# Six layers on one core: the latent attention layer computed with tokens on partitions

## What is computed

```
def mla_mixer(xn, positions, w_in, q_lat_norm, kv_lat_norm, w_uq, w_ukv, q_norm, k_norm, w_out):
    cq, ckv, kr, z = jnp.split(xn @ w_in, cuts, axis=-1)      # widths 384, 256, 32, 1024
    q = (rmsnorm(cq, q_lat_norm) @ w_uq).reshape(bsz, seq, 16, 96)
    kv = (rmsnorm(ckv, kv_lat_norm) @ w_ukv).reshape(bsz, seq, 16, 64 + 64)
    k_nope, v = kv[..., :64], kv[..., 64:]
    k = jnp.concatenate([k_nope, broadcast(kr)], axis=-1)     # 64 + 32 = 96
    q, k = rmsnorm(q, q_norm), rmsnorm(k, k_norm)
    # rope on the last 32 of the 96 of q and of k
    o = dense_chunk_attention(q, k, v, 96 ** -0.5)            # key chunk of 64 <= query chunk
    return (o * jax.nn.silu(z)) @ w_out
```

## Time and profile before

| | |
|---|---|
| median of 3 runs | 1074.57 us |
| profiled execution, its own time | 1076.47 us |
| its span, first to last instruction | 1074.7 us |
| mean granted TensorE clock | 0.954 of full |
| TensorE busy | 994.5 us (93%) |
| VectorE busy | 647.7 us (60%) |
| ScalarE busy | 496.2 us (46%) |
| GpSimd busy | 337.5 us (31%) |
| DMA | 148.5 MB, mean 138 GB/s |

### The profile page before, as it was taken

One profiled execution on the slowest core, in us unless ns is written; L12 is line 12 of the kernel. 1 busy time (PEld: TensorE's weight loads), 2 busy tenths in 40 slices (PEclk: granted clock), 3 DMA queues, 4 the chain that ended last, 5 costly groups with the idle time before them and its releaser, 6 DMA issues.

```text
span 1074.7 us, 17517 instructions
## 1 busy us (share of the span) xinstructions
PE 994.5 (93%) x7143; PEld 920.9 (86%) x7143; DVE 647.7 (60%) x1000; ACT 496.2 (46%) x668; POOL 337.5 (31%) x270
## 2 busy tenths in 40 slices
PE   6999958988869999988999999899999999999798
PEld 5999947677759988855999999899999997988698
DVE  5777535895585553558367665878665544555632
ACT  5553335444674345237244345334445236474521
POOL 7442652441122110713044323866401100222400
PEclk9999979999989999659999999899999999999998
DMA  9884424324222324503249553445464552424400
GB/s 252 211 224 167 155 76 173 128 108 157 79 82 100 119 62 133 164 6 79 57 122 234 169 215 126 157 143 190 179 235 157 194 206 78 157 86 150 157 1 40
DMA packets 128022, 148.49 MB, mean 138 GB/s; under 512 B 12835, under 2 KB 83760, under 8 KB 127952
## 3 DMA queue, kind: packets, MB, share of 16 engines
q1 hardware_dynamic: 127248, 146.32, 42.4%
q0 software_dynamic: 448, 1.12, 0.4%
q10 hardware_dynamic: 256, 0.07, 0.0%
HBM read 146.44 MB, written 1.05 MB: 137 GB/s over the span
## 4 chain that ended last, share of the span: by engine, by line
PE 61%; DVE 8%; ACT 6%; POOL 3%; issue 2%; DVEq 0%; ACTq 0%; POOLq 0%
PE acc L1557 39%; PE aux L1557 21%; POOL arena L1428 1%; DVE wlo L812 1%; ACT whi L444 1%; POOL arena L1429 1%; POOL arena L1427 1%; ACT arena L470 1%; DVE wlo L831 1%; DVE score L1109 1%; DVE work L1153 1%; DVE top L1108 1%; ACT work L656 1%; DVE arena L918 1%; ACT work L663 0%
## 5 line engine op out<-in xcount | busy, mean ns | idle before, releaser
L812 DVE TENSOR_TENSOR wlo<-raw,whi 128x2048 fp32r<-128x2048 f32 (+5 forms) x128 | 286.3, 2264 | 138.1 <-ACT whi L436 136.1
L1557 PE MATMUL acc<-xh,whi 128*128 128x256 f32 (+1 forms) x1208 | 346.4, 287 | 7.8 <-DVE wlo L812 4.2
L1557 PE MATMUL acc<-xh,wlo 128*128 128x256 f32 (+1 forms) x1208 | 343.6, 284 | 0.0
L1557 PE MATMUL acc<-xl,whi 128*128 128x256 f32 (+1 forms) x1208 | 343.6, 284 | 0.0
L436 ACT ACTIVATE whi<-raw 128x2048 fp32r<-128x2048 f32 (+5 forms) x128 | 207.5, 1653 | 107.8 <-PE aux L1557 60.4
L1557 PEld LDWEIGHTS acc<-xh,whi 128*128 128x128 f32 (+1 forms) x1208 | 233.1, 193 | 10.2 <-issue 5.8
L1557 PEld LDWEIGHTS acc<-xl,whi 128*128 128x128 f32 (+1 forms) x1208 | 233.2, 193 | 0.0
L1557 PEld LDWEIGHTS acc<-xh,wlo 128*128 128x128 f32 (+1 forms) x1208 | 233.0, 193 | 0.0
L1557 PE MATMUL aux<-yh,whi 128*128 128x256 f32 x352 | 99.9, 284 | 0.0
L1557 PE MATMUL aux<-yl,whi 128*128 128x256 f32 x352 | 99.6, 283 | 0.0
L1557 PE MATMUL aux<-yh,wlo 128*128 128x256 f32 x352 | 99.6, 283 | 0.0
(11 more groups left out here) (293 smaller groups left out, 1784.3 us busy)
## 6 DMA issues: line engine op xcount, KB each, us to landing
raw<-in_a_w_in SPq DMA_DIRECT2D x52, 512.0 KB, 6.6
raw<-in_sb_w_in SPq DMA_DIRECT2D x48, 512.0 KB, 5.6
raw<-in_b_w_in SPq DMA_DIRECT2D x36, 512.0 KB, 5.5
raw<-in_pool_w_in SPq DMA_DIRECT2D x32, 512.0 KB, 6.0
raw<-in_a_w_out SPq DMA_DIRECT2D x16, 512.0 KB, 5.0
raw<-in_pool_w_out SPq DMA_DIRECT2D x16, 512.0 KB, 5.2
raw<-in_sb_w_out SPq DMA_DIRECT2D x16, 512.0 KB, 5.0
raw<-in_c_w_in SPq DMA_DIRECT2D x12, 512.0 KB, 5.6
```

Source lines behind the costliest of these rows:

```text
L812: TT(wlo[b][:, lo:hi], (raw_third if third else raw[b])[:, lo:hi], whi[b][:, lo:hi].bitcast(F32), ALU.subtract).then_inc(lo_ready, 1)
L1557: return nc.tensor.matmul(out_, lhsT, rhs, start=start, stop=stop, skip_group_check=True)
```

## The change

The latent layer is computed with tokens on partitions. The latents (C0 with the columns 336 to 671, C0+1 with 0 to 335) come out as 128 tokens by 336 columns; squares are summed along rows by the accumulator of ScalarE; the factors are one number per partition; ten transposes bring the normed latents back to feature-major, where they are the stationary operand for k, v and q. The up-projections are eight events of 512 columns (four heads of k and v) and eight of 384 (four heads of q), token block by token block. ScalarE evacuates the first token block and VectorE the second; squares on ScalarE, sums by head with a reduction on VectorE, Ln and Exp in place of the square root; GpSimd applies the factor of k, writes the shared rotary part into every head and does the rope of q. Sixteen groups of four transposes bring k and q to 96 rows by 256 tokens, with the gain applied in the copy out. The heads take the paired form of the sparse layer (`paired_heads` for both); the last four groups of transposes, the second half of z (C0+7) and half of the first output unit stand between them as fillers, and the splits of the two output units are spread over them by quarters. The layer has 10 units for 14. The second angle table and its two constants, the rotation matrices and the first 128 KB broadcast of the positions go; two small gain loads and nine small operations on GpSimd come.

The core of the diff. The counterpart on VectorE of ScalarE's part has the same order and is not shown; what is removed can be seen in the functions above.

```diff
-A0, B0, C0, A1, P0, S0, END = 0, 10, 22, 36, 46, 62, 78
+A0, B0, C0, A1, P0, S0, END = 0, 10, 22, 32, 42, 58, 74
...
-        shapes = {B0 + 1: (8, 72), C0 + 2: (8, 160)}
-        for u in range(C0 + 4, C0 + 8):
-            shapes[u] = (2, 512)
-        for u in range(C0 + 8, C0 + 12):
-            shapes[u] = (3, 384)
+        shapes = {B0 + 1: (8, 72), C0: (8, 336), C0 + 1: (8, 336), C0 + 3: (2, 2048), C0 + 4: (3, 768),
+                  C0 + 5: (3, 384), C0 + 6: (3, 384)}
...
+        MLA_SPLITS = {first + q: (u, q) for first, u in ((2, C0 + 8), (11, C0 + 9)) for q in range(4)}
...
-            plain(C0, w, 0, 0)
-            plain(C0 + 1, w, 0, 672)
-            plain(C0 + 2, w, 0, 512)
-            plain(C0 + 3, w, 0, 1184)
-            for n in range(4):
-                plain(C0 + 4 + n, a["c_w_ukv"][0], 0, 512 * n)
-            for n in range(4):
-                plain(C0 + 8 + n, a["c_w_uq"][0], 0, 384 * n)
+            plain(C0, w, 0, 336)
+            plain(C0 + 1, w, 0, 0)
+            plain(C0 + 2, w, 0, 672)
+            plain(C0 + 3, a["c_w_ukv"][0], 0, 0)
+            plain(C0 + 4, a["c_w_uq"][0], 0, 0)
+            plain(C0 + 5, a["c_w_uq"][0], 0, 768)
+            plain(C0 + 6, a["c_w_uq"][0], 0, 1152)
+            plain(C0 + 7, w, 0, 1184)
             for h in range(2):
-                plain(C0 + 12 + h, a["c_w_out"][0], 4 * h, 0)
+                plain(C0 + 8 + h, a["c_w_out"][0], 4 * h, 0)
...
+            split(C0 + 2, (0,))
+            for t in range(NT):
+                latent_square(t, t, 48, 304, 0)
+            for t in range(NT):
+                latent_square(t, t, 304, 336, 1)
+            root(2, log=True)
+            for t in range(NT):
+                latent_square(t, t, 0, 48, 2)
+            split(C0 + 2, (1,))
+            act.wait_ge(unit_done, C0 + 2)
+            for t in range(NT):
+                latent_square(t, 2 + t, 0, 336, 3)
+            log_root(lms[:, :], lfac[:, :], "lat_ms", 1, "lat_root")
+            split(C0 + 3, (0,))
+            act.wait_ge(sem("lat_f"), 1)
+            A(lat[:, 0, 384:640], acc[:, 0, 48:304], ACT.Copy, scale=lfac[:, 0:1])
+            A(krs[:, 0, :], acc[:, 0, 304:336], ACT.Copy, scale=rT[:, 4:5])
+            A(lat[:, 0, 336:384], acc[:, 0, 0:48], ACT.Copy, scale=lfac[:, 2:3])
+            A(lat[:, 0, 0:336], acc[:, 2, 0:336], ACT.Copy, scale=lfac[:, 2:3]).then_inc(sem("lat_a"), 1)
+            split(C0 + 3, (1,))
...
+            split(C0 + 4)
             silu(40, 4, 3)
...
+            nc.scalar.preload_act_table_set("natural_log_exp_and_others")
+            for c in range(4):
+                name, count = kv_signal(2 * c)
+                act.wait_ge(sem(name), count)
+                src = c_bank(2 * c).rearrange("p (h d) -> p h d", d=128)
+                h = 4 * (c % 2)
+                A(kfull[2 * (c // 2)][:, h:h + 4, 0:64], src[:, :, 0:64], ACT.Copy).then_inc(sem("k_raw_a"), 1)
+                A(vC[:, 0, 256 * c:256 * c + 256].rearrange("p (h d) -> p h d", d=64), src[:, :, 64:128], ACT.Copy)\
+                    .then_inc(sem("kv_out_a"), 1)
+                for t in range(NT):
+                    e = 2 * c + t
+                    act.wait_ge(sem("k_raw_v" if t else "k_raw_a"), c + 1)
+                    if e >= 4:
+                        act.wait_ge(sem("k_summed"), e - 3)
+                    A(k_square(e).rearrange("p (h d) -> p h d", d=64), kfull[2 * (c // 2) + t][:, h:h + 4, 0:64],
+                      ACT.Square).then_inc(sem("k_squared"), 1)
+                if c == 2:
+                    log_root(c_heads(0, 1, 0), c_heads(1, 1, 0), "k_ms", 1, "k_root")
...
+            for c in range(4):
+                name, count = q_signal(2 * c)
+                act.wait_ge(sem(name), count)
+                h, g = 4 * (c % 2), c // 2
+                src = c_bank(8 + 2 * c)[:, 0:W384].rearrange("p (h d) -> p h d", d=96)
+                A(qraw[2 * g][:, h:h + 4, :], src, ACT.Copy).then_inc(sem("q_out_a"), 1)
                 for t in range(NT):
...
+                    act.wait_ge(sem("q_out_v" if t else "q_out_a"), c + 1)
+                    if c:
+                        act.wait_ge(sem("q_summed"), 2 * c - 1 + t)
+                    A(work[:, 4 + t, :].rearrange("p (h d) -> p h d", d=96), qraw[2 * g + t][:, h:h + 4, :], ACT.Square)\
+                        .then_inc(sem("q_squared"), 1)
+                if c == 0:
+                    log_root(c_heads(0, 1, 1), c_heads(1, 1, 1), "k_ms", 2, "k_root")
+                if c == 1:
+                    split(C0 + 6)
+                if c == 2:
+                    log_root(c_heads(0, 0, 0), c_heads(1, 0, 0), "q_ms", 1, "q_root")
+                    turn_copy(0)
+                    turn_copy(2)
+            turn_copy(4)
+            log_root(c_heads(0, 0, 1), c_heads(1, 0, 1), "q_ms", 2, "q_root")
+            turn_copy(6)
+            turn_copy(8)
+            turn_copy(10)
+            split(C0 + 7)
+            softmax_heads(1)
...
+            pool.wait_ge(sem("lat_a"), 1)
+            pool.wait_ge(sem("lat_v"), 1)
+            sin = c_tab[:, 1, 1, :, :]
+            TT(krt[:, :, 0:16], krs[:, :, 16:32], sin[:, :, 0:16], ALU.mult)
+            me.link(TT(krt[:, :, 16:32], krs[:, :, 0:16], sin[:, :, 16:32], ALU.mult))
+            me.link(TT(krs[:, :, :], krs[:, :, :], c_tab[:, 1, 0, :, :], ALU.mult))
+            me.link(TT(krs[:, :, :], krs[:, :, :], krt[:, :, :], ALU.add))
+            for g in range(2):
+                pool.wait_ge(sem("k_factor"), g + 1)
+                for t in range(NT):
+                    k, f = kfull[2 * g + t], c_heads(1, 1, g)[:, t, :].rearrange("p (h d) -> p h d", d=1)
+                    TT(k[:, :, 0:64], k[:, :, 0:64], f.broadcast_to([P, 8, 64]), ALU.mult)
+                    TT(k[:, :, 64:96], over_heads(krs[:, t, :]), f.broadcast_to([P, 8, 32]), ALU.mult)\
+                        .then_inc(sem("k_done"), 1)
+            for g in range(2):
+                for t in range(NT):
+                    pool.wait_ge(sem("q_squared"), 4 * g + 3 + t)
+                    q = qraw[2 * g + t][:, :, 64:96]
+                    cos, sin = c_tab[:, 0, 0, t, :], c_tab[:, 0, 1, t, :]
+                    TT(qturn[:, :, 0:16], q[:, :, 16:32], over_heads(sin[:, 0:16]), ALU.mult)
+                    me.link(TT(qturn[:, :, 16:32], q[:, :, 0:16], over_heads(sin[:, 16:32]), ALU.mult))
+                    me.link(TT(q, q, over_heads(cos), ALU.mult))
+                    TT(q, q, qturn[:, :, :], ALU.add).then_inc(sem("q_done"), 1)
+                    pool.wait_ge(sem("q_done"), 2 * g + t + 1)
...
+            def mla_filler(f):
+                if f < 2:
+                    turn_heads(12 + 2 * f)
+                    turn_heads(13 + 2 * f)
+                if f in (5, 6, 8, 9):
+                    if f == 5:
+                        taken("turn_out_v", 7)
+                        taken("turn_out_a", 8)
+                    unit(C0 + 7, in_tiles(1), xh, xl, part=(2 * (5, 6, 8, 9).index(f), 2))
+                if f in (12, 13, 15, 16):
+                    if f == 12:
+                        taken("z_raw", 4)
+                    attention_out(C0 + 8, 16, (12, 13, 15, 16).index(f), 0)
+            def turn_heads(i):
+                if 4 <= i < 12:
+                    taken("turn_out_v" if i % 2 else "turn_out_a", (i - 4) // 2 + 1)
+                elif i > 12:
+                    taken(*((), ("turn_out_a", 6), ("turn_out_v", 6), ("turn_out_a", 7))[i - 12])
+                g = i % 8 // 4
+                o, src = turn_bank(i), (kfull if i < 8 else qraw)[2 * g:2 * g + 2]
+                for n in range(2):
+                    for t in range(NT):
+                        ins = nc.tensor.transpose(o[0:96, T * n + t * P:T * n + t * P + P], src[t][:, 2 * (i % 4) + n, :], ident)
+                ins.then_inc(sem("head_turned"), 1)
...
+            token_unit(C0, x_wait(2))
+            token_unit(C0 + 1, sums_late)
+            unit(C0 + 2, [(aux_tile(4 + n), P * n, P) for n in range(4)], xh, xl, latent_turns)
+            def latent_event(e, u, n0, kn, c, width):
+                wh, wl = w_view(u, *unit_shape(u))
+                tok = slice(e % 2 * P, e % 2 * P + P)
+                for k in range(kn):
+                    if c == 0 and e % 2 == 0 and k in (0, (kn + 1) // 2):
+                        pe.wait_ge(lo_ready, 2 * u + 1 + (k > 0))
+                    ins = three(c_bank(e)[:, 0:width], yh[:, n0 + k, tok], yl[:, n0 + k, tok], wh[:, k, c:c + width],
+                                wl[:, k, c:c + width], k == 0)
+                return ins
+            taken("latl_ready", 2)
+            for e in range(8):
+                if e == 2:
+                    taken("z_raw", 3)
+                if e >= 4:
+                    taken("kv_out_v" if e % 2 else "kv_out_a", e // 2 - 1)
+                ins = latent_event(e, C0 + 3, 3, 2, 512 * (e // 2), 512)
+                ins.then_inc(sem(kv_signal(e)[0]), 1)
+            taken("latl_ready", 5)
```

(23 more changed lines are left out.)

## The result

On one chip, in four executions each, the changed kernel took 1007.77 us in the median (1006.14 to 1010.85) and the kernel before 1074.76 (1072.35 to 1077.69): ratio 0.9379, 95% interval 0.9345 to 0.9412. The profiled execution took 1006.14 us, span 1004.2, where the sum had 1025.6.

What follows compares the result with a forecast made beforehand. TensorE's side work was taken to bound the latent layer's first stage. First stage 74, heads 53 and output 17.3 gave 144.3 for 195.2 us, 50.9 less: median 1024, range 1010 to 1036 with 0.66.

Steps and rivals of the forecast that it cites:

- Edits at nothing: Outside the layer: angle table leaving GpSimd and ScalarE, small table products coming, counted 0; 3 or 4 us if cover gone.
- What bounds the kernel: First stage worth what TensorE does in it; norm and rope products hold 41.0 of its 131.6 us.
- cross-check from the other side: First stage from 131.6 less removed work plus 6.4 for transposes: 65.6, against 69 built up from new work.
- Latents 17, z unit 30, k and v 43: First stage, ends in us after layer start: latents 17, z unit C0+2 30, k and v (C0+3) 43.
- q 58, turns 61.5, split 69: First stage, ends after layer start: q 58, thirty-two further head transposes 61.5, split of second z unit 69 us.
- 5 us added for contention and clock: First stage: 69 raised to 74 for small ops and splits beside GpSimd and a low clock after TensorE's wait.
- rival 1: First stage: VectorE and GpSimd in each other's way; GpSimd ends at 56 to 84, time 1034 to 1048, chance 0.14.
- Heads 53: Heads last 53 us for 40.3 before, taken between 57.7 from the sparse heads and 49.5 followed step by step.
- Output 17.3: Output products after the heads: 144 products, 17.3 us for 23.2.
- 2: Heads: low clock stays from transposes through first four pairs and their z products, 12 us more, 1036, chance 0.07.
- 3: TensorE bound everywhere, split hidden better: first stage 64, heads 49, time 1009, chance 0.08.
- 4 and 5: 4: GpSimd in series before the heads, 1092, chance 0.03; 5: longer heads lose the first stage's gain, 1074, chance 0.02.

Runs made afterwards that it cites:

- the three moves: Changed kernel with C0+7's split quartered into heads 0 to 3, first SiLU behind split(C0+5), last unit's quarters one head later: 1004.1 us, 0.9317; again 1003.49 us, 0.9319.

## Why the prediction was wrong, and where it was right

**The step that failed is "Edits at nothing".** It said of the 256-column angle table that goes and the small products that come that "both lie where GpSimd otherwise waits, and the sparse layer's start hangs on ScalarE and VectorE", and that if that cover were gone it would be 3 or 4 us. The first half looked at GpSimd's idle time. The second half named ScalarE as what the start hangs on and did not look at what ScalarE waited for: GpSimd, for 18.83 us. The step costed the work where it is done, and not the place of the wait for its result in the other engine's program. Measured price: 15 to 20 us with the chain cut in the kernel before, 13.9 (9 to 19) with it put back in the changed one, where the sum had 0. Had the waits of the stretch in which a removed line stands been read, with the line that waits for the removed chain (L522, 18.8 us) as the first of them, some 16 us could have been in the sum.

**What bounds the kernel: right in direction, too round in size.** TensorE's side products did bound the first stage for the most part, but cutting them to a stub gave 19 of its 62.8 us. The 41.0 was a sum of durations, which overlap, while the prices beside it are distances between starts; by distances it is some 34. The sum did not lean on that: it was built up from the new work. The cross-check from the other side did take 41.0, and gave 65.6 beside 69 with one term too large by some 7; that it came near is luck, and it was no independent check.

**Latents 17, z unit 30, k and v 43.** 15.7, 28.7 and 41.2. (The terms of the first add up to 16.0; 1 us in its 17 has no source.) The latent chain is done at 22 after the start of the layer, forecast 24, and TensorE does not wait for it. The SiLU ahead of the k evacuation costs TensorE 1.2 for the 1.5 in the sum.

**q 58, turns 61.5, split 69.** The twelfth group of transposes is over near 62.4, and the first score is taken up at 68.8. The chain of the changed kernel there is the one that the prediction described:

```profile
384.45 0.64 PE aux L1909 x4
385.09 0.50 PE acc L1909 x4
...
385.64 0.56 issue
386.20 1.91 ACT whi L456
...
388.13 4.49 DVE wlo L862 x2
392.63 0.20 DVE work L1155
```

TensorE's wait is 5.0 us, of the 5 to 9 forecast; taking the split out gave 5.4 us in the first stage and 3.0 in the layer.

**The 5 us added for contention and clock: not there.** The splits beside GpSimd took 2.27 and 2.11 where the row had 3.00 and alone 1.43, 1.5 us in all, and a pair of 8-column steps took 1.09 beside it and 0.36 alone, another 0.7; not only the splits suffer. The clock of the whole stage is 0.98. That allowance is the largest error inside the layer, 5.2 of the first stage, and it was taken from the worst row. GpSimd's 512-column steps were 1.04 or 1.05 in three of four cases and 1.83 in one, its end at 386.8, 63 after the start, inside the 56 to 84 of rival 1 and never waited for.

**Heads 53.** 54.4. The 53 was picked between two workings, 57.7 and 49.5, so that it came near is in part luck. The 1.2 us of the table loads at head 11 are about the difference; the sum had no term for them.

**Output 17.3 and behind it nothing.** 17.5, and 539.7 for 539.1.

**Rivals.** 1: out, as said. 2: seen over the first 15 or 16 us of the heads, at 0.58 in the run without rope, with 3.5 us and not 12, and at 0.78 and 0.63 in the two executions of the three moves; it was 0.89 or 0.90 in both executions of the changed kernel. The Trainium skill (TensorE: Matmul & The Clock Gate, Part 4: PE-mode transpose) says that transposes don't count as PE busy in the way that raises the clock. The rows neither bear it out nor refute it: after the same transposes the clock was 0.89 or 0.90 twice behind a gap of 5.0 us, and 0.58 once behind one of 6.3. 3: its 1009 (its terms give 1010) is near the time that came, but not for its reason; the first stage was 68.8 and not 64, the heads 54.4 and not 49. With that and the chain it would have been 992. 4 and 5: not seen.

## What to carry to other kernels

An edit that removes work is worth what waits for it, and the wait can stand anywhere in another engine's program: look up who reads the result, then where that engine's wait stands in its program, and what is queued behind it. A table that is wanted 240 us later had cost some 16 us. Moving its wait behind the next layer's first steps, the cheapest fix, gave 11 of them (7 to 15); the rest hung on a sum that stood behind the same chain on GpSimd. And when one engine's side work is cut, only as much comes out as the next engine allows: taking 22 to 25 us from TensorE gave 19, and the other engines' half another 10.

## What was not expected of the hardware

- A VectorE step of 32 columns with all operands in SBUF took 1.19 and 1.30 us beside GpSimd for 0.19 alone, and ended with GpSimd's instruction. The prediction had the row of a long split for such contention, 3.00 for 1.43; a short step can be stretched sixfold. The Trainium skill (SBUF — State Buffer, Who interferes with whom) says that VectorE with two SBUF inputs contends with a GpSimd instruction that reads SBUF, and these rows agree. It says of the 2-port modes that the other engine is blocked for the whole instruction; here a `SCALAR_TENSOR_TENSOR` is held to the end too.
- The start of the latent layer scattered from 322.0 to 327.9 us over seven profiled executions of kernels that are the same up to there; in the three latest (327.6 and later) the granted clock between 130 and 160 us was 0.89, in the earliest 1.00. So of the 16.6 us read from two executions up to 4 may be the execution's. By the ratios of the medians the chain is worth 9 to 20 us.
- A product with 16 columns kept 306 and 303 ns of busy time where one with 256 had 422 and 385, at a granted clock of 0.67 and 0.66 over 424 us to the stage's end. By distance from start to start, in a stretch without waits of each, it is 0.16 us with 16 columns and 0.21 with 256: a sixteenth of the columns saves a quarter of the time.

```profile
440.24 0.30 PE L1557 MATMUL aux<-fl,ident 16*96 16x16 f32 x1
440.40 0.30 PE L1557 MATMUL aux<-fh,ident 16*96 16x16 f32 x1
...
453.95 0.41 PE L1557 MATMUL aux<-fh,ident 16*96 16x256 f32 x1
454.16 0.41 PE L1557 MATMUL aux<-fl,ident 16*96 16x256 f32 x1
```
